# Beginning every on-chip tile on a multiple of 64 bytes in place of 32, in a three-block model kernel

## The reference

```python
x = first_block(x, ...)    # rms norm, w_in, 31-tap causal conv + S5 state scan, two gated outputs, w_out
for layer in range(2):     # second_block
    x = x + 0.5 * _swiglu(_rmsnorm(x, g[0]), w_gate[layer, 0], w_up[layer, 0], w_down[layer, 0])
    h = _rmsnorm(x, g[1])
    mix = _conv_rwkv_mixer(h, ...) if layer % 2 == 0 else _mla_mixer(h, cos, sin, ...)
    x = x + mix
    x = x + 0.5 * _swiglu(_rmsnorm(x, g[2]), w_gate[layer, 1], w_up[layer, 1], w_down[layer, 1])
```

## The kernel before

| operand | remainder |
|---|---|
| every moving tile: hH, hL, ffn_aH, ffn_aL, st_hi, st_lo, mixH, mixL, yH, yL, mH, mL, o_hi, o_lo, cq, cv | 32 |
| weights of all units: w_hi, w_lo | 0 |
| gate and up weights, high: v even / v odd | 32 / 0 |
| gate and up weights, low: v % 3 = 0, 1 / 2 | 32 / 0 |

## Time and profile before

### The profile page before, as it was taken

One profiled execution on the slowest core, in us unless ns is written; L12 is line 12 of the kernel. 1 busy time (PEld: TensorE's weight loads), 2 busy tenths in 40 slices (PEclk: granted clock), 3 DMA queues, 4 the chain that ended last, 5 costly groups with the idle time before them and its releaser, 6 DMA issues.

```text
span 2443.8 us, 42260 instructions
## 1 busy us (share of the span) xinstructions
PE 2379.5 (97%) x16963; PEld 2001.1 (82%) x16963; DVE 1738.9 (71%) x2296; ACT 1148.6 (47%) x1758; POOL 879.2 (36%) x533
## 2 busy tenths in 40 slices
PE   8999999999999999989999999999999999999999
PEld 6666767789899777877998998998987557898997
DVE  6999986496485589766864867855846676883771
ACT  5533353465364346244652645643644344662552
POOL 3799934322313456422123123132134212114123
PEclk9999999999999999999999999999999999999999
DMA  5222224233343432002434342342423221333333
GB/s 149 78 78 78 74 65 130 60 93 104 99 111 84 112 93 67 27 4 57 121 84 115 104 121 78 92 124 79 111 85 98 51 57 53 87 94 108 102 89 94
DMA packets 420791, 214.48 MB, mean 88 GB/s; under 512 B 17317, under 2 KB 419035, under 8 KB 420603
## 3 DMA queue, kind: packets, MB, share of 16 engines
q1 hardware_dynamic: 416523, 209.05, 31.1%
q10 hardware_dynamic: 4080, 2.83, 0.5%
HBM read 209.22 MB, written 2.10 MB: 86 GB/s over the span
## 4 chain that ended last, share of the span: by engine, by line
PE 85%; DVE 9%; ACT 3%; issue 2%; POOL 1%; DMA 0%; ACTq 0%; DVEq 0%; POOLq 0%
PE bank L337 11%; PE bank L334 11%; PE bank L330 11%; PE bank L987 11%; PE bank L992 10%; PE bank L995 10%; PE bank L1848 3%; PE bank L1852 3%; PE bank L1855 3%; DVE bank L1682 3%; PE bank L3392 1%; PE bank L2740 1%; PE bank L3458 1%; DVE hL L361 1%; PE bank L2720 1%
## 5 line engine op out<-in xcount | busy, mean ns | idle before, releaser
L312 POOL TENSOR_TENSOR w_lo<-w_raw,w_hi 128x1024 fp32r<-128x1024 f32 (+5 forms) x276 | 532.4, 1931 | 631.9 <-ACT w_hi L304 630.2
L304 ACT ACTIVATE w_hi<-w_raw 128x1024 fp32r<-128x1024 f32 (+5 forms) x276 | 237.7, 861 | 649.0 <-PE bank L337 486.4
L584 DVE TENSOR_TENSOR gu_w_lo<-gu_w,gu_w_hi 128x1024 fp32r<-128x1024 f32 (+1 forms) x256 | 365.2, 1429 | 99.6 <-ACT gu_w_hi L575 99.0
L656 POOL TENSOR_TENSOR ffn_aL<-tmp,ffn_aH 128x512 fp32r<-128x512 f32 x88 | 134.6, 1529 | 739.5 <-ACT ffn_aH L700 739.5
L575 ACT ACTIVATE gu_w_hi<-gu_w 128x1024 fp32r<-128x1024 f32 (+1 forms) x256 | 303.2, 1186 | 3.0 <-DVE gu_w L558 3.0
L692 ACT ACTIVATE tmp<-bank 128x256 f32<-128x256 f32 x320 | 121.6, 380 | 191.0 <-PE bank L995 187.5
L987 PE MATMUL bank<-hH,gu_w_hi 128*128 128x256 f32 x1280 | 205.1, 282 | 4.8 <-ACT tmp L692 4.8
L992 PE MATMUL bank<-hL,gu_w_hi 128*128 128x256 f32 x1280 | 204.0, 282 | 0.0
L995 PE MATMUL bank<-hH,gu_w_lo 128*128 128x256 f32 x1280 | 204.0, 282 | 0.0
L960 DVE TENSOR_TENSOR bank<-bank,R 128x512 f32<-128x512 f32 x64 | 44.8, 699 | 212.9 <-PE bank L337 212.0
L330 PE MATMUL bank<-ffn_aH,w_hi 128*128 128x512 f32 x704 | 185.2, 395 | 0.0
(11 more groups left out here) (553 smaller groups left out, 4707.7 us busy)
## 6 DMA issues: line engine op xcount, KB each, us to landing
gu_w<-in_ffn_w_gate SPq DMA_DIRECT2D x88, 512.0 KB, 4.0
gu_w<-in_ffn_w_up SPq DMA_DIRECT2D x88, 512.0 KB, 5.3
w_raw<-in_w_in SPq DMA_DIRECT2D x48, 512.0 KB, 3.8
w_raw<-in_ffn_w_down SPq DMA_DIRECT2D x64, 384.0 KB, 3.4
w_raw<-in_ffn_w_down SPq DMA_DIRECT2D x64, 320.0 KB, 3.2
w_raw<-in_even_w_in SPq DMA_DIRECT2D x26, 512.0 KB, 3.8
w_raw<-in_w_conv_out SPq DMA_DIRECT2D x8, 512.0 KB, 3.8
w_raw<-in_w_out SPq DMA_DIRECT2D x8, 512.0 KB, 3.8
```

The lines of the kernel that those rows point to most:

```text
L304: nc.scalar.activation(w_hi[u % 2][:, 0:K, :], w_raw[u % 4][:, 0:K, :], ACT.Identity).then_inc(w_hi_ready, 1)
L312: nc.gpsimd.tensor_tensor(w_lo[u % 2][:, 0:K, :], w_raw[u % 4][:, 0:K, :], w_hi[u % 2][:, 0:K, :].bitcast(F32), ALU.subtract).then_inc(w_l ...
L584: nc.vector.tensor_tensor(gu_wl[v % 3][:, b0:b1, :, :], gu_w[v % 3][:, b0:b1, :, :], gu_wh[v % 2][:, b0:b1, :, :].bitcast(F32), ALU.subtra ...
L656: nc.gpsimd.tensor_tensor(aL[:, in_half(n), :], up_t[:, :], aH[:, in_half(n), :].bitcast(F32), ALU.subtract).then_inc(a_lo, 1)
```

## The change

One line of `Map.put` rounds a tile's size up to 64 bytes in place of 32.

```diff
@@ -86,7 +86,7 @@
                 n = 4
                 for s in shape[1:]:
                     n *= s
-                self.at += (n + 31) // 32 * 32
+                self.at += (n + 63) // 64 * 64
                 assert self.at <= end0, (name, self.at, end0)
                 return t
```

## The result

The changed kernel takes 2423.11 us (median of 4 runs, 2420.58 to 2424.27) beside 2445.80 us for the kernel before (4 runs, 2443.03 to 2448.66): a ratio of 0.9904, with a 95% interval of 0.9892 to 0.9916. The profiled execution spans 2421.6 us, 22.2 us less than the one of before. It is faster, by more than the 14.7 us that were forecast, and within the range.

A forecast was written before the change was run, and what follows sets the result against it. The prediction took TensorE, matmul count times pitch, as the bound: 2443.8 - 24.1 (units) + 9.8 (gate and up tiles) - 0.4 (plain tiles) = 2429.1 us, with a range from 2412 to 2455 us.

The forecast's parts named there:

- TensorE's pitch is the time: For most of the span TensorE has its operands ready; time is the number of matmuls times their pitch.
- The pitch depends on the distance between the two streams' addresses: Weight loads and column streaming collide by address distance: equal remainders 226.7 ns at 512 columns, 120.0 at 256; unequal 233.3, 116.7.
- (b): Rival: the weights' own address counts; units stay at 233.3 ns, all gate and up tiles take 9.80 us; 2432.3 us; chance 0.10.
- (c): Rival: straddling 64-byte boundaries costs; without it pitches fall to 220 and 113.3 ns; 2360 us; chance 0.12.
- Modulo 64: Weights-to-activations distance counts modulo 64, since 480 bytes gives 0.93 us for four matmuls, as 32 does.
- rival (a): Nothing changes, 2443.8 us: place in memory counts, or a distance of 64 acts like 32; chance 0.18.
- Part 1: 512-column units go from 233.3 to 226.7 ns: -24.1 us, between -15.2 and -28.6.
- parts 1 and 3: Units with 512 columns speed up, -24.1 us; plain tiles lose unequal distances on 56 matmuls, -0.4 us.
- Part 2: Gate and up tiles, 256 columns, all go to 120.0 ns, 10.08 us a tile: +9.8 us, ends 0 and +9.8.
- The pair stage hides its gain: Convolution and scan stage: VectorE busy 60.00 of 60 us, so 5.1 us gained on 768 matmuls is hidden, priced at nothing.
- Other engines and DMAs at nothing: VectorE sums, ScalarE splits, GpSimd and DMAs at new addresses: no effect taken; ends 0.01 us an instruction, some 256 splits.
- Rival (d): Slower: the bad case of each length, gate and up tiles 120.0 ns, units 233.3 ns; 2454.5 us; chance 0.14.

The follow-up runs named there:

- D = 0: Kernel before with the parameter tile cut to 504 columns, so activations stand 0 bytes from the ring's weights modulo 256: 2433.80 us, ratio 0.9960.
- D = 256: Kernel before with the parameter tile cut to 440 columns, so activations stand 256 bytes from the ring's weights: 2432.76 us, ratio 0.9959.
- D = 96: Kernel before with a 64-byte gap behind `small`, so activations stand 96 bytes past the ring's weights modulo 256: 2453.87 us in a single run.
- D = 160: Kernel before with the parameter tile cut to 416 columns, so activations stand 160 bytes past the ring's weights modulo 256: 2451.81 us, single run.

## Why the prediction was right, and where it was not

*TensorE's pitch is the time.* Right. 15.2 of the 22.2 us are read from pitches in the down projections and the tiles. The other 7.0 lie where the units' matmuls fell from 233 to 229 ns too, and the counts of instructions did not change (16963 matmuls in both).

*The pitch depends on the distance between the two streams' addresses.* Right, and shown by the run with the base up by 32 (nothing changes) and those with D = 0 and D = 256. This was also what spoke against rivals (b), the weights' own address, and (c), straddling a 64-byte boundary: tiles 4 and 6 keep 10.08 us when all their operands move from 32 to 0 modulo 64.

*Modulo 64.* This is the step that failed. It rested on one comparison, a distance of 32 and one of 480 with the same pitch. The period is 256, 480 is 224, and 224 and 32 happen to have the same pitch of 233.3 ns. So a distance of 64 was no return to 0 but a value of its own, which no row of the kernel before contained. The prediction named this in rival (a), but with the pitches of 32 as the only alternative. By its own signs, runs of five were to start 1.13 us apart and start 1.145, and six tiles were to read 10.08 us, of which two do.

*Part 1, units: -24.1 us.* Measured 16.0 (9.0 on the down projections, 7.0 elsewhere, with the plain tiles). The sign is right, the size off: the pitch fell by 4.3 ns in place of 6.6. At the distance that was assumed, the run with D = 0 gave 22.2 for parts 1 and 3 together. There the eight down projections gave 13.2 (forecast 13.9) and all else 9.1 (forecast 10.6, with two thirds of the units that share their stage let through), so that share was about right.

*Part 2, gate and up tiles: +9.8 us.* Measured -6.2: the wrong sign, by the same step. At D = 0 it was 9.6, so the term was sized well. One count was off without harm: six of the 80 tiles are longer for a wait (10.4 to 14.6 us before), not two or so.

*The sum.* -14.7 forecast, -22.2 measured. Two errors from one cause, 8.5 too much gain (24.5 against 16.0) and 16.0 too much loss (9.8 against -6.2), cancelled in part. That the forecast's time came within 6 us is luck to that extent.

*The pair stage hides its gain.* Right, 262.20 us twice. That VectorE holds it is less sure. VectorE's tap on line 1682 (232 of them write a bank) takes 769 ns in median before, 750 in the changed kernel and 815 at D = 0, and the stage lasts 262.2, 262.2 and 261.8 us: these durations alone do not set its length. GpSimd's difference on line 312 stays at 2402, 2404 and 2398 ns. GpSimd is busy 231.9 of 262.2 us there, and in the changed kernel the chain that ended last runs mostly through it. The chain's shares in the stretch from 100 to 300 us, of the kernel before:

```profile
by line: PE bank L1848 16.9%; PE bank L1852 15.9%; DVE bank L1682 15.1%; PE bank L1855 15.0%; issue 4.2%; PE bank L1936 3.7%; POOL w_lo L312 3.6%; PE bank L1947 2.5%; PE bank L1949 2.2%; DVE tmp L1710 1.7%; DVE bank L1698 1.5%; DVE bank L17
```

Of the changed kernel:

```profile
by line: POOL w_lo L312 27.1%; POOL tmp L1310 7.8%; POOL tmp L1315 7.5%; POOL tmp L1313 7.5%; POOL ph_sin L1296 6.2%; POOL tmp L1304 6.0%; POOL tmp L1306 5.8%; PE bank L1848 4.8%; PE bank L1852 4.6%; PE bank L1855 4.6%; issue 4.0%; POOL s_i
```

TensorE has all but left the chain there; no run tells GpSimd from VectorE as the one that holds it.

*Other engines and DMAs at nothing.* Right for the time: VectorE's sums on line 556 kept theirs, and TensorE's longest waits in total (8.2 us for ScalarE before, 8.6 after) point to no other term. That VectorE's durations do not depend on the layout is not right: see the tap above.

*Rival (d), slower.* D = 96 is a case of it, with both of its pitches (233.4 ns, and 10.07 us for tile 5) and 2453.9 us in one run, where 2454.5 was its price; D = 160 took 2451.8 us, also in one run. Slower was possible, one step of 32 bytes past the change.

The Trainium skill, "SBUF — State Buffer", gives 16-byte lines (section "Specifications (TRN2)") and two independent read ports of TensorE (section "Who interferes with whom"). By these all kernels here would take one time. They spread from 2414.9 to 2453.9 us, by addresses alone, all on multiples of 32.

What stays open: why the period is 256 bytes, whether weight loads and matmuls collide at all, as the prediction took it (the runs vary the distance and see the pitch, and nothing between), why a stream of 256 columns has two pitches at distances 32 and 64, and what brings the fast one back.

## What to carry to other kernels

Where fp32r matmuls follow one another and each loads its weights, as here, the pitch depends on the distance of the two addresses modulo 256, and on the number of columns; alignment to 64 bytes as such did nothing. Other types were not run. Read the pitch for each pair of buffers from the starts in the timeline, over several buffers with different remainders, before a layout is taken as given; where the trace has only a few distances, a distance it lacks is unknown, and a short sweep of one padding settles it. Two lengths of matmul can want two distances (here 0 for 512 columns and 32 or 64 for 256), and giving each its own took the kernel to 2414.9 us, 1.3% under the kernel before. The pitch that is best in single tiles (113.3 ns at 64) was not the best for the kernel: at it the matmuls caught up with the engine that empties their banks, and fell to 117.6.

## What the runs showed of the hardware that was not expected

- The pitch of fp32r matmuls at full clock has a period of 256 bytes in the distance between stationary and moving operand: 227.0 to 234.3 ns with 512 columns, 113.3 to 120.0 with 256.
- The direction counts: 64 above gives 229.0 ns, 64 below (192) 233.3.
- In steady stretches the distance between single starts repeats in a short cycle: 226, 227, 227 ns at a distance of 0; 231, 232, 237 at 96; 231, 236 at 192.
- At one and the same layout the stream of 256-column matmuls can run at 113.3 or at 117.6 ns, the slower one for nearly the whole kernel, at another at 116.7 or 117.6 for whole halves, with nothing waited for meanwhile. Each of the seven falls from 113.3 to 117.6 ns within tiles 5 and 6 came at a wait of well under 0.1 us for ScalarE (at 552.16 us: 177 ns between two starts, in place of 113). The list of waits does not show one so short; the starts do.
